# Feed-forward operands: block sums taken from transposed blocks, 64 transpositions in place of 112

## The reference

```
h = rms_norm(x) * (1 + sc1) + sh1;  x = x + g1 * mlstm_mixer(h)
h = rms_norm(x) * (1 + sc2) + sh2
gate, up = split(h @ w_gate_up)          # 1024 -> 2 x 2816
x = x + g2 * ((silu(gate) * up) @ w_down)
return rms_norm(x) * final_norm_w
```

## Time and profile before

| | |
|---|---|
| median of 3 runs | 1117.61 us (1117.46 to 1118.28) |
| the profiled execution | 1117.69 us, of which the span of its instructions 1115.9 us |
| busy PE / DVE / ACT / POOL | 1093.0 / 693.0 / 429.6 / 184.3 us |
| granted TensorE clock | 0.999 in the mean |

### The profile page before, as it was taken

The page is one execution under the profiler, slowest core; times in us unless marked ns, Lnnn a source line. Parts: engine busy times, 40 slices in busy tenths (PEclk is TensorE's granted clock), DMA queues, the critical chain, the costliest instruction groups (busy, mean ns, idle before and its releaser), DMA issues.

```text
span 1115.9 us, 15219 instructions
## 1 busy us (share of the span) xinstructions
PE 1093.0 (98%) x5517; PEld 927.9 (83%) x5517; DVE 693.0 (62%) x1171; ACT 429.6 (38%) x767; POOL 184.3 (17%) x152
## 2 busy tenths in 40 slices
PE   4999999999999999999999999999999999999997
PEld 4799888888888899988888888888888888888886
DVE  5957745455456735776676767566766564944676
ACT  6772321321222522453333333333333334544344
POOL 5633312212325532730000000000000000000000
PEclk9999999999999999999999999999999999999999
DMA  9415633432531532112646354536443779755653
GB/s 367 166 59 176 187 93 95 146 95 76 156 114 57 192 111 95 77 38 79 214 156 202 101 192 149 186 100 217 142 157 136 265 262 390 250 189 190 198 159 151
DMA packets 87194, 178.17 MB, mean 160 GB/s; under 512 B 8120, under 2 KB 31288, under 8 KB 86096
## 3 DMA queue, kind: packets, MB, share of 16 engines
q1 hardware_dynamic: 86416, 175.07, 46.3%
q0 software_dynamic: 704, 2.13, 0.6%
HBM read 137.02 MB, written 40.16 MB: 159 GB/s over the span
## 4 chain that ended last, share of the span: by engine, by line
PE 56%; DVE 1%; ACT 0%; issue 0%; DVEq 0%
PE OP L2081 26%; PE O L2081 15%; PE ST L2081 5%; PE DC L2081 5%; PE AD L2081 5%; PE ST L1863 0%; PE O L1863 0%; DVE hL L1245 0%; DVE x L1708 0%; DVE tL L1245 0%; DVE x L1715 0%; ACT junk L1029 0%; DVE x L1698 0%; ACT hH L1023 0%; DVE sB L1667 0%
## 5 line engine op out<-in xcount | busy, mean ns | idle before, releaser
L1834 PE MATMUL OP<-wH,hH 128*128 128x256 f32 (+1 forms) x448 | 151.1, 337 | 0.8 <-DVE hL L1348 0.8
L1834 PE MATMUL OP<-wH,hL 128*128 128x256 f32 (+1 forms) x448 | 147.5, 329 | 0.0
L1834 PE MATMUL OP<-wL,hH 128*128 128x256 f32 (+1 forms) x448 | 147.4, 329 | 0.0
L1617 DVE TENSOR_TENSOR dL<-dF,dH 128x1024 fp32r<-128x1024 f32 x77 | 93.0, 1223 | 69.9 <-ACT dH L1077 69.0
L1077 ACT CAST dH<-dF 128x1024 fp32r<-128x1024 f32 x77 | 79.8, 1052 | 89.0 <-DMA dF<-w_units 40.3
L2081 PE MATMUL OP<-tH,wsH 128*128 128x512 f32 x264 | 103.1, 390 | 0.0
L2081 PE MATMUL OP<-tL,wsH 128*128 128x512 f32 x264 | 102.9, 390 | 0.0
L2081 PE MATMUL OP<-tH,wsL 128*128 128x512 f32 x264 | 102.9, 390 | 0.0
L1834 PEld LDWEIGHTS OP<-wH,hH 128*128 128x128 f32 x448 | 85.1, 190 | 7.8 <-DVE hL L1348 1.0
L1834 PEld LDWEIGHTS OP<-wH,hL 128*128 128x128 f32 x448 | 85.0, 190 | 7.8
L1834 PEld LDWEIGHTS OP<-wL,hH 128*128 128x128 f32 x448 | 85.2, 190 | 6.8
(11 more groups left out here) (311 smaller groups left out, 2695.6 us busy)
## 6 DMA issues: line engine op xcount, KB each, us to landing
raw<-w_units SPq DMA_DIRECT2D x76, 512.0 KB, 4.6
dF<-act_mid SPq DMA_DIRECT2D x77, 256.0 KB, 2.7
ada<-ada_rest SPq DMA_DIRECT2D x64, 256.0 KB, 2.9
wst<-w_units SPq DMA_DIRECT2D x44, 256.0 KB, 4.8
down_mid<-wst SPq DMA_DIRECT2D x22, 512.0 KB, 3.2
dF<-down_mid SPq DMA_DIRECT2D x44, 256.0 KB, 2.9
dF<-w_units SPq DMA_DIRECT2D x33, 256.0 KB, 5.9
ada<-ada_first SPq DMA_DIRECT2D x8, 1024.0 KB, 10.3
```

The source lines that it names most:

```text
L1617: nc.vector.tensor_tensor(dL[g][:], dF[g][:], dH[g][:].bitcast(F32), ALU.subtract).then_inc(d_L, 1)
L1834: ins = nc.tensor.matmul(out_ap, lhs[a], rhs[b], start=(n == 0 and i == 0), stop=(last and i == 2))
```

## The change

The transposition comes before the sums. Every row tile's half is transposed once (16 groups, 64 transpositions: Q11, Q21 of tiles 0 to 3, Q12, Q22 of tiles 4 to 7). ACT copies each transposed group from PSUM back into SBUF, to the place of its rows in x2 (copy_rows, new semaphore n_cp); with that the bank is free. POOL makes the four sums from these transposed blocks, and high and low read the blocks and the sums from SBUF. The sums of a tile wait for n_cp in place of n_sh. The list of splits (HL_FIRST, HL_AFTER) is now separate from that of transpositions. Waits that guarded memory by n_tr are now on n_L or n_cp.

```diff
+def row_tiles(p):
+    t = TOKENS[p]
+    return [("Q11", t), ("Q21", t)] if t < 4 else [("Q12", t), ("Q22", t)]
 def operand_tiles(p):
-    return [("Q11", t), ("Q21", t)] if t < 4 else [("Q22", t)]
+    return [e for e in row_tiles(p) if e[0] != "Q12"]
 def transpose_plan():
+    first = {4: row_tiles(0), 6: row_tiles(1), 8: row_tiles(2), 10: row_tiles(3), 12: row_tiles(4), 14: row_tiles(5),
+             15: row_tiles(6)}
+    after = {1: row_tiles(7)}
+    return first, after
+def split_plan():
     first = {4: operand_tiles(0), 6: operand_tiles(1), 8: operand_tiles(2), 10: operand_tiles(3),
              11: [("T1", 4), ("T2", 4)], 12: operand_tiles(4), 14: operand_tiles(5), 15: [("T1", 5), ("T2", 5)]}
-    after = {0: [("T3", 4), ("T3", 5)], 1: [("Q22", 6), ("T1", 6), ("T2", 6)], 2: [("T1", 7), ("Q22", 7), ("T2", 7)],
-             3: [("T4", 4), ("T4", 5)], 4: [("T3", 6), ("T3", 7)], 5: [("T4", 6), ("T4", 7)]}
+    after = {0: operand_tiles(6) + [("T3", 4), ("T3", 5)], 1: operand_tiles(7) + [("T1", 6), ("T2", 6)],
+             2: [("T1", 7), ("T2", 7)], 3: [("T4", 4), ("T4", 5)], 4: [("T3", 6), ("T3", 7)], 5: [("T4", 6), ("T4", 7)]}
...
 operand_sums (POOL):
-                pool.wait_ge(n_sh, p + 1)
+                pool.wait_ge(n_cp, max(TR_AT["Q22", t], TR_AT["Q21", t - 4]) + 1)
...
-                    pool.wait_ge(n_tr, 2 * NT + TR_AT["T2", UPPER[i - 2]] + 1)
+                    pool.wait_ge(n_L, HL_AT["T2", UPPER[i - 2]] + 1)
...
 ACT:
+            def copy_rows(entries):
+                for kind, t in entries:
+                    e = TR_AT[kind, t]
+                    act.wait_ge(n_tr, 2 * NT + e + 1)
+                    nc.scalar.copy(operand_rows(kind, t), TR_BANKS[e % 3][:]).then_inc(n_cp, 1)
...
-                    act.wait_ge(n_tr, 2 * NT + e + 1)
+                    if kind[0] == "Q":
+                        act.wait_ge(n_cp, TR_AT[kind, t] + 1)
+                    else:
+                        act.wait_ge(t_sum, 4 * UPPER.index(t) + int(kind[1]))
...
-                                   TR_BANKS[e % 3][:].rearrange("p (k n) -> p k n", n=P)).then_inc(n_H, 1)
+                                   operand_rows(kind, t).rearrange("p (k n) -> p k n", n=P)).then_inc(n_H, 1)
...
 copy_p2:
+                if n < 2:
+                    act.wait_ge(n_L, HL_AT["T2", 5] + 1)
 copy_p5:
+                if n == 0:
+                    act.wait_ge(n_L, HL_AT["T2", 6] + 1)
...
-                high(TR_FIRST.get(2 * p, ()))
+                copy_rows(TR_FIRST.get(2 * p, ()))
+                high(HL_FIRST.get(2 * p, ()))
...
             copy_p2(0)
-            high(TR_AFTER[1])
+            copy_rows(TR_AFTER[1])
+            high(HL_AFTER[1])
...
 low (DVE):
-                                            TR_BANKS[e % 3][:].rearrange("p (k n) -> p k n", n=P),
+                                            operand_rows(kind, t).rearrange("p (k n) -> p k n", n=P),
...
 up_sum (DVE, n = 1):
-                    row_of = {5: ("T1", 4), 6: ("T4", 4), 7: ("T4", 5), 3: ("T4", 6)}[q]
-                    dve.wait_ge(n_tr, 2 * NT + TR_AT[row_of] + 1)
+                    row_of = {5: ("T2", 4), 6: ("T4", 4), 7: ("T4", 5), 3: ("T4", 6)}[q]
+                    dve.wait_ge(n_L, HL_AT[row_of] + 1)
...
 transposes2 (PE):
-                    if kind[0] == "Q":
-                        pe.wait_ge(n_sh, PLACE[t] + 1)
-                    else:
-                        pe.wait_ge(t_sum, 4 * UPPER.index(t) + int(kind[1]))
+                    pe.wait_ge(n_sh, PLACE[t] + 1)
                     if e >= 3:
-                        pe.wait_ge(n_L, e - 2)
+                        pe.wait_ge(n_cp, e - 2)
```

More of the change, by code:

```diff
@@ L93 @@
 TR_AT = {e: n for n, e in enumerate(TR_SEQ)}
+HL_FIRST, HL_AFTER = split_plan()
+HL_SEQ = [e for m in sorted(HL_FIRST) for e in HL_FIRST[m]] + [e for m in sorted(HL_AFTER) for e in HL_AFTER[m]]
+HL_AT = {e: n for n, e in enumerate(HL_SEQ)}
 UP_SEQ = up_sequence()
@@ L277, in build @@
         y_mm, y_ev = sem("y_mm"), sem("y_ev")
-        t_sum = sem("t_sum")
+        t_sum, n_cp = sem("t_sum"), sem("rows_transposed_copied")
         c_sum, c_H, c_L, up_mm = sem("c_sum"), sem("c_H"), sem("c_L"), sem("up_mm")
@@ L324, in kind_done, with operand_rows @@
         def kind_done(kind):
-            return max(n for (k, _), n in TR_AT.items() if k == kind) + 1
+            return max(n for (k, _), n in HL_AT.items() if k == kind) + 1
+        def operand_rows(kind, t):
+            if kind == "T2":
+                return t2[UPPER.index(t) % 2][:]
+            row, part = {"Q11": (t, 0), "Q21": (t, 1), "Q12": (t, 0), "Q22": (t, 1), "T1": (t, 0), "T3": (t - 4, 0),
+                         "T4": (t - 4, 1)}[kind]
+            return x2[:, row, part * HALF:(part + 1) * HALF]
         def l_count(n, q):
@@ L498, in load_chunk @@
                 else:
-                    sp.wait_ge(n_tr, 2 * NT + len(TR_SEQ))
+                    sp.wait_ge(n_L, HL_AT["T2", 7] + 1)
                 g, cols = n // 2, slice(n % 2 * CHUNK, (n % 2 + 1) * CHUNK)
@@ L763, in operand_sums @@
                 if i >= 2:
-                    pool.wait_ge(n_tr, 2 * NT + TR_AT["T2", UPPER[i - 2]] + 1)
+                    pool.wait_ge(n_L, HL_AT["T2", UPPER[i - 2]] + 1)
                 pool.wait_ge(t_sum, 4 * i + 1)
                 nc.gpsimd.tensor_tensor(t2[i % 2][:], b1_, b0, ALU.subtract).then_inc(t_sum, 1)
-                pool.wait_ge(n_tr, 2 * NT + TR_AT["Q11", t - 4] + 1)
+                pool.wait_ge(n_L, HL_AT["Q11", t - 4] + 1)
                 pool.wait_ge(t_sum, 4 * i + 2)
                 nc.gpsimd.tensor_tensor(a0, t2[i % 2][:], a0, ALU.subtract).then_inc(t_sum, 1)
-                pool.wait_ge(n_tr, 2 * NT + TR_AT["Q21", t - 4] + 1)
+                pool.wait_ge(n_L, HL_AT["Q21", t - 4] + 1)
                 nc.gpsimd.tensor_tensor(a1, a1, t2[i % 2][:], ALU.subtract).then_inc(t_sum, 1)
@@ L1011, in up_cast @@
                 elif n == 1 and q == 4:
-                    act.wait_ge(n_tr, 2 * NT + TR_AT["T4", 7] + 1)
+                    act.wait_ge(n_L, HL_AT["T4", 7] + 1)
                 nc.scalar.copy(wsH[n % 2][W_SLOT.index(q)][:], src).then_inc(c_H, 1)
-            def high(entries):
+            def copy_rows(entries):
                 for kind, t in entries:
@@ L1019, in high @@
                     act.wait_ge(n_tr, 2 * NT + e + 1)
+                    nc.scalar.copy(operand_rows(kind, t), TR_BANKS[e % 3][:]).then_inc(n_cp, 1)
+            def high(entries):
+                for kind, t in entries:
[3 more added lines that the diff above has]
+                        act.wait_ge(t_sum, 4 * UPPER.index(t) + int(kind[1]))
                     if kind == "T3" and t == 4:
@@ L1109, in _ @@
                 row_root(NT + p, NT + t)
-                high(TR_FIRST.get(2 * p + 1, ()))
+                copy_rows(TR_FIRST.get(2 * p + 1, ()))
+                high(HL_FIRST.get(2 * p + 1, ()))
                 if p == 3:
@@ L1113, in _ @@
                     up_cast(1, 1)
-            high(TR_AFTER[0])
+            high(HL_AFTER[0])
             copy_p2(0)
-            high(TR_AFTER[1])
+            copy_rows(TR_AFTER[1])
+            high(HL_AFTER[1])
             silu0(0)
             copy_p2(1)
-            high(TR_AFTER[2])
+            high(HL_AFTER[2])
             silu0(1)
-            high(TR_AFTER[3])
+            high(HL_AFTER[3])
             up_cast(1, 5)
             copy_p5(0)
-            high(TR_AFTER[4])
+            high(HL_AFTER[4])
             copy_u2(0)
-            high(TR_AFTER[5])
+            high(HL_AFTER[5])
             for q in (6, 7):
@@ L1720, in _ @@
                     norm_row(p - 1)
-                low(TR_FIRST.get(2 * p, ()))
+                low(HL_FIRST.get(2 * p, ()))
                 y_tile(2 * NT + 2 * p + 1)
@@ L1728, in _ @@
                 row_inverse(NT + p, NT + t)
-                low(TR_FIRST.get(2 * p + 1, ()))
+                low(HL_FIRST.get(2 * p + 1, ()))
             norm_row(NT - 1)
-            low(TR_AFTER[0])
+            low(HL_AFTER[0])
             add_c11(0)
-            low(TR_AFTER[1])
-            low(TR_AFTER[2])
+            low(HL_AFTER[1])
+            low(HL_AFTER[2])
             add_c11(1)
-            low(TR_AFTER[3])
+            low(HL_AFTER[3])
             up_sum(1, 5)
@@ L1740, in _ @@
             up_low(1, 5)
-            low(TR_AFTER[4])
-            low(TR_AFTER[5])
+            low(HL_AFTER[4])
+            low(HL_AFTER[5])
             up_sum(1, 3)
@@ L1852, in transposes2 @@
                     e = TR_AT[kind, t]
-                    if kind[0] == "Q":
-                        pe.wait_ge(n_sh, PLACE[t] + 1)
-                    else:
-                        pe.wait_ge(t_sum, 4 * UPPER.index(t) + int(kind[1]))
+                    pe.wait_ge(n_sh, PLACE[t] + 1)
                     if e >= 3:
-                        pe.wait_ge(n_L, e - 2)
-                    row, part = {"Q11": (t, 0), "Q21": (t, 1), "Q22": (t, 1), "T1": (t, 0), "T3": (t - 4, 0),
```

(6 more changed lines are left out.)

6 lines of the change are left out of this document (1 added, 5 removed).

## The result

The changed kernel takes 1138.34 us in the median (1136.56 to 1139.63, 5 runs) against 1117.53 (1117.37 to 1118.28, 5 runs): ratio 1.0184, 95% interval 1.0173 to 1.0196. It is 20.8 us slower; 14 had been forecast, and the time lies 0.3 us above the range. The profiled execution took 1138.34 us with a span of 1136.5.

What follows compares the result with a forecast made beforehand. PE, 98% busy, was taken as the bound: stalls 18.65 less transpositions 5.2 less present holes 1.2 gives 12.2 (walk 12.05); 1117.7 + 12.05 + 2 for the clock = 1131.7, stated as 1131.5 us, range 1122 to 1138.

Steps and rivals of the forecast that it cites:

- The saving, 12 groups at 0.43: Transposition groups on PE among the products fall from 14 to 2, saving 5.2 us, all behind 473.5 us.
- The wait on POOL ahead of the shifts: POOL's sums wait for transposition and copy, delaying shift(3) and shift(5) behind them, which PE's places 10 and 14 need.
- The first hole: Before place 10: PE waits for POOL's shift(3), sums starting at 450.05; a stall of 5.0 us.
- Second and third: PE stalls before place 14, for shift(5), 4.75 us, and before tile 7's transpositions, for DVE's shift(7), 4.6 us.
- Fourth and fifth: PE stalls before product (0, 5), for T1's low, 2.25 us, and before (0, 7), for T3's lows, 2.05 us.
- TensorE's clock: Slow work behind PE's three long stalls: 0 to 7.5 us possible, at most 2.5 a spell; 2 us taken, one spell.
- Rival 2: The clock falls in all three long stalls: 12.05 + 7.5, 1137 us; chance 0.16.
- The lows held by POOL: DVE's low subtractions with two SBUF inputs each wait for one POOL sum, 1.29 us.
- Rival 1: The lows are not held by POOL: stalls shrink, 6.0 us later, 1124 us; chance 0.16.
- Rival 3: POOL's order does not bite: 5.2 saved less 1.75 for T3's chain, 1114.3 us; chance 0.04.
- rival 4: Only the first stall bites: 4.65 later at place 10, then 4.7 less and 1 us of chain, 1118.7; chance 0.06.
- The edits costed at nothing: Waits moved to n_cp or n_L on load_chunk, up_cast(1, 4), up_sum(1, ...), copy_p2 and copy_p5: no cost.

Runs made afterwards that it cites:

- e12: e11 plus a second wait on POOL: the sums of tile 6 start only behind DVE's shift of tile 7; 1118.52 us (1.0012 to the kernel before).
- e3_wait_alone: Kernel before the change, with only the sums of tiles 4 and 5 also waiting behind the tile's transposition; no copies; 1128.98 us (1.0106).
- e1_pool_order: Changed kernel, POOL's list reordered: shift(3) ahead of the sums of tile 4, shift(5) ahead of those of tile 5; 1129.85 us (1.0109).
- e4_psum_splits: Changed kernel, with high and low of the Q blocks reading the PSUM bank again; 1134.63 us (1.0154 to the kernel before).
- e2_fill: Changed kernel with 60, 40 and 40 extra identity transpositions ahead of PE's waits for tiles 2, 3 and 7; 1132.12 us (1.0131).
- e8_wait_fill: e3_wait_alone with 44 and 34 extra identity transpositions ahead of PE's waits for tiles 2 and 3; 1125.57 us (1.0071).
- e6: e5, but high and low of the Q blocks read SBUF as in the changed kernel; 1130.18 us (1.0113 to the kernel before).
- e5: Changed kernel, POOL's shifts 3 to 5 moved ahead of sums, Q splits from PSUM, T1, T2 splits moved, T3 of tiles 6, 7 earlier; 1123.31 us (1.0051).
- e7: e5, but T4 of tiles 4, 5, weight sums and cast of unit (1, 5) again ahead of T3 of tiles 6, 7; 1123.26 us (1.0052).
- e9: e5, with tile 5's sums waiting for tile 6's shift, sums of tiles 6, 7 made by kind, tile 7 copied ahead of copy_p2(0); 1122.09 us (1.0040).
- e10: e9 without the wait for tile 6's shift ahead of the sums of tile 5; 1124.59 us (1.0062 to the kernel before).
- e11: e9, with T3 of tiles 6, 7 split ahead of silu0(1), add_c11(1) and T4, and copy_u2(0) ahead of a weight cast; 1120.94 us (1.0033).

## Why the prediction came out as it did

- **What bounds the kernel: right.** The loss of 20.7 us is there in full at product (0, 7), and holes and slow spells on PE account for it to about half a microsecond (next point).
- **The saving, 12 groups at 0.43: its size was not measured by itself, but the sums close with it.** PE is due one pitch behind the start of its last matmul, which makes a hole some 0.16 us longer than the idle figure. Changed kernel: holes from due time 7.2 + 4.9 + 4.8 + 0.9 + 2.0 = 19.8, spells 7.9, less 5.2, less the 1.2 of before, gives 21.3 for 20.7 found; the 0.6 between them is open. For e12: holes 0.2 + 0.8 + 2.7 + 1.8, from due time about 6.1, a spell of 1 to 1.5, less 6.4 (5.2 and 1.2), gives about 1; found is 0.8 in the spans.
- **The wait on POOL ahead of the shifts: right.** Place, releaser and order of the three long holes are as forecast; e3_wait_alone shows the first two without anything else of the change; with POOL's order alone mended, e1_pool_order cuts the first to 1.4 and takes the second away, but moves 3.2 us to place 12.
- **The first hole: the term "stall of 5.0 us" was mis-sized, 7.2 measured.** The step "ACT starts 0.63 us behind a group (435.00 and 435.63): 448.87, then 449.36, done 449.95" failed. It took ACT to be free; but the rule I had just applied to the lows beside POOL's sums holds for the lows of places 4 and 6 beside POOL's shifts too (3.5 us for 1.28). They held y_tile, y_tile held the square, and the square held the copies, done at 452.2. e4_psum_splits gives this back. The cue was in the earlier trace rows: a low at 443.42 beside a shift at 443.58, which the prediction read only for what it shows of a low out of PSUM.
- **Second and third: 4.75 and 4.6 forecast, 4.9 and 4.8 from due time measured. Fourth and fifth: 4.3 together forecast, 2.9 measured**: PE came slow into that stretch, so the chains had time. With PE at full pace there (e2_fill) the fourth is 2.5 from due time, near the 2.25 forecast.
- **TensorE's clock: the step that failed most. "I take 2 us, one spell" was mis-sized, 7.9 measured, three spells of 2.5 to 2.8.** The price of one spell (at most 2.5) was nearly right, the count was not: I took the low end because full-pace work surrounds each hole, and that protected none of the three. The windows show the clock at 0.50 behind the first hole and 0.54 behind the third. The Trainium skill, "TensorE: Matmul & The Clock Gate", Part 1, has idleness lower the clock and work restore it. The trace agrees, by the same windows: 0.50 behind the hole, 1.00 six microseconds later. The prediction had this only as its second rival. e2_fill and e8_wait_fill show the price by taking it away.
- **The lows held by POOL: right.** A low takes 1.75 at 454.57 beside sums and 0.68 at 500.22 with POOL idle; e6 against e5 prices the reading out of SBUF at 6.9 us with the orders mended. Rival 1 is refuted. The Trainium skill, "SBUF — State Buffer", section "Who interferes with whom", has a VectorE instruction with two SBUF inputs contend with a GpSimd instruction that reads SBUF. The trace agrees, by the same two rows.
- **Rival 2 (1137) was the case that came**, with 2.2 us more in the first hole and 1.4 less in the last two; that these nearly cancel is luck. Rival 3 needed POOL's order not to bite, and rival 4 only the first hole; three came. Even with many orders mended (e12) the 5.2 us are spent. The likely reason, argued from e12's rows and not tested by itself, is that for the last tiles the chain of transposition, copy, sum, cast and split is longer than the products that should cover it. That no order can do better is not shown; e12's holes still sum to 5.5 us.
- **The edits costed at nothing: one was wrong in e5, none in the change.** In e5 copy_p2(0), through its new wait on T2's low, held ACT 5.6 us (copy at 486.78) and tile 7's copies behind it. In the changed kernel the same wait held it for 1.1 us (copy at 495.98) with no effect on PE, which waited elsewhere.

## What to carry to other kernels

Where an engine works in order, look at what stands behind a wait before moving it: here four sums were delayed by 6 us, and it was the shift behind them that PE needed. Put side by side what is saved on the engine that bounds the kernel and the chain that now has to fit under its work; here 5.2 us of transpositions were saved, and the price was a longer way through ACT, POOL and DVE for every tile. Price a hole on PE of some microseconds with the slow work behind it, and when an operand moves from PSUM to SBUF, go through every place where GpSimd is busy beside the VectorE instruction that reads the operand, not only the ones under study.

## What the runs showed of the hardware

- The slow spells behind holes of 7.0, 4.7 and 4.7 us cost 2.8, 2.6 and 2.5 us, so hardly depend on the hole's length there; the granted clock is 0.50 behind the first and 0.54 behind the third. Even behind the hole of 2.69 us in e12 the first matmul takes 0.77 us, against 0.47 where the clock holds (510.10, behind a hole of 0.76). The length of a hole does not settle it alone: before place 15, e5 and e7 both idle 2.7 us, and the first 128x512 matmul behind (475.94 and 475.87) takes 0.76 in e5 and 0.47 in e7 (granted clock from 475 to 480 us 0.66 and 1.00). What decides between them is open.
- Useless transpositions in the holes made two kernels faster, by 6.2 and 3.4 us, with the granted clock at 1.00 from 440 to 520 us.
- VectorE, with two SBUF inputs, and GpSimd take turns by whole instructions: a low of 0.68 takes up to 1.8 beside sums, and some 2.8 beside a shift (an estimate from 3.49 for two, less one undisturbed). A wait that keeps POOL out of DVE's way gained 2.5 (e9 against e10) and 2.4 us (e12 against e11).
- In the first 30 us of the trace the granted clock reads 1.00 while PE works slowly; in mid-kernel the reading and the pace agree.
